# Two attention mixers rewritten: heads in pairs on halves of the array, query norms in the exponent's scale, output units between the pairs

## Chip, core and metric

The kernel runs on one core of one Trainium2 chip. The time is that of the device for one execution, in microseconds; the median of the runs is what counts. TensorE is PE (its weight load PEld), VectorE is DVE, ScalarE is ACT, GpSimd is POOL, SyncE is SP.

## What is computed

Two transformer stacks one after the other on a stream of 256 tokens by 1024 features. The change touches only the mixer of the first stack, which runs twice (two layers). Cut to the mixer:

```python
proj = h @ w_in[l]                      # 1024 -> 1888
a, b_q, b_k, b_v, c, d_cq, d_ckv, d_kr = split(proj)
# a: gated, depthwise convolution of 31 taps, layer norm, silu
o_a = silu(layer_norm(conv31(a[:256] * sigmoid(a[256:])), ln_a_g, ln_a_b))
# b: 4 query heads of 64, 2 key/value heads, RMS norm of q and k, rotary
q = rope_2d(rms_norm(b_q, qk_norm_q)); k = rope_2d(rms_norm(b_k, qk_norm_k))
o_b = softmax(q k^T / 8) v
# c: spatial gating
u, s = gelu(c); s = layer_norm(s) * g + b; o_c = u * (sgu_w @ s + sgu_b)
# d: latent attention, 4 heads of 64 + 32 rotary features
qd = rms_norm(d_cq, mla_q_norm) @ w_uq; kvd = rms_norm(d_ckv, mla_kv_norm) @ w_ukv
o_d = softmax(q_full k_full^T / sqrt(96)) v_d
h = layer_norm(alpha * h + concat(o_a, o_b, o_c, o_d) @ w_out)
```

All is float32. The large projections split each operand into a high and a low float32r part and take three matmuls per product (hi*hi, hi*lo, lo*hi).

## The kernel before

Every engine has its own program in hand-written order, and semaphores tie them together. `mixer(l)` exists once per engine.

**Weights.** They come in units of 128 x 2048 floats (1 MB) in a ring of three buffers. A unit is loaded by SP when the unit three before it has been split; ACT's `split()` copies the raw unit to `w_hi` (line 1473), DVE's `split()` subtracts it to give `w_lo` (line 2038), and PE uses both. ACT's and DVE's splits stand in program order among all their other work, and the n-th split of DVE waits for the n-th of ACT. A mixer has eight input units (`in0` to `in7`, order `IN_ORDER`), one raw unit with the small latent and gating weights (`mla`), four output units (`out0` to `out3`, order `OUT_ORDER`), and then the feed-forward's `gate0` and `up0`.

**Input side.** PE makes `a`, its gate, `q`, `k`/`v`, the latents `cq` and `ckv`, `u` and `sv` (lines 681 and 690, 48 or 72 matmuls each). ACT copies `q`, `k` and the latents out of PSUM and squares them; PE sums the squares with constant matrices (1039, 1041, 1054 to 1056); ACT takes square roots; DVE takes reciprocals of 128 x 768 and 128 x 512 (2436, 2445) and scales `q`, `k` and the latents. Then come rotary matmuls (1061 to 1068), transposes of the gating weights (1079), latent up-projections (1086 to 1101) and their rotary part (1109, 1112), which DVE finishes (2038, from 139 to 144.7 us in the first mixer).

**Attention.** Eight heads go one by one: PE scores (979, two matmuls), DVE maximum (2373) and its negative (2378), ACT exponent with the sum (1689), DVE reciprocal and scaling of the probabilities (2384, 2387), PE transposes (990), ACT copy, PE values (1003), ACT result into `mix`. Behind heads 0 to 4 DVE lays the last 18 of the 30 convolution taps that follow the first (`more_taps`, 2035: a tap is two operations of 128 x 256, and a turn of the loop is two taps), PE lays the gating product `branch_c` behind head 2 (1126, 1127) and the mean and variance of branch a behind heads 5 and 8 (1135, 1142).

**Output.** After the last head `out_rows` runs the four output units (833, 24 matmuls of 128 x 512 each) in the order 1, 2, 0, 3: unit k takes two tiles of `mix`, which DVE splits into `act_hi` and `act_lo` (`split_operand`, 2073 and 2038). Tiles 0 and 1 are branch a, 2 and 3 the heads of b, 4 and 5 branch c, 6 and 7 the heads of d.

## Time and profile before

| | us |
|---|---|
| median of 3 runs | 1941.95 (1940.13 to 1942.10) |
| profiled execution, its own time | 1947.68 |
| its span | 1945.9 |
| PE busy | 1867.0 (96%) |
| DVE busy | 1265.8 (65%) |
| ACT busy | 898.9 (46%) |
| POOL busy | 109.9 (6%) |
| granted TensorE clock, mean | 0.975 |

PE's share is high, but "busy" counts a matmul at half clock as much as one at full clock. The first mixer runs from 74 to 213 us, the second from 413 to 551 us, 339 us later and alike to within a microsecond. Where several engines hand small pieces to each other, the time is read from the order of the pieces, not from the shares.

### The profile page before, as it was taken

The numbers are of one execution on the slowest core, as the hardware profiler recorded it, in microseconds if no ns is written. First come the engines' busy times: TensorE is split into PE (matmuls) and PEld (weight loads), VectorE is DVE, ScalarE is ACT, GpSimd is POOL, SyncE is SP. The second block draws the span as 40 slices with busy tenths as digits, with TensorE's granted clock in tenths as the row PEclk, the third lists the DMA queues.
The fourth block names the chain that finished last, engine by engine and source line by source line (L and its number), as shares of the span: only waits on it lengthen the run. The fifth ranks groups of instructions, "written<-read, shape, count | busy, mean of one in ns | idle before, by whom it ended". The sixth has DMA issues, their size and how long they took to land.

```text
span 1945.9 us, 31345 instructions
## 1 busy us (share of the span) xinstructions
PE 1867.0 (96%) x12538; PEld 1681.6 (86%) x12551; DVE 1265.8 (65%) x1569; ACT 898.9 (46%) x1082; POOL 109.9 (6%) x79
## 2 busy tenths in 40 slices
PE   6988999998999998999999999999999998899999
PEld 6975899987589997999898888999999987789998
DVE  5786877788787677555667655555655567556555
ACT  5544544444454445333554455333433357545332
POOL 0300200030020000000034000000000000000000
PEclk9996999999699999999999999999999998999999
DMA  9540465554046554555442544555555542335553
GB/s 299 187 140 13 145 223 178 175 162 147 8 146 217 193 176 134 191 193 177 132 148 87 202 166 138 188 193 180 177 194 176 190 152 87 110 107 174 183 183 129
DMA packets 227044, 311.34 MB, mean 160 GB/s; under 512 B 6614, under 2 KB 199414, under 8 KB 226326
## 3 DMA queue, kind: packets, MB, share of 16 engines
q1 hardware_dynamic: 224038, 298.07, 45.9%
q0 software_dynamic: 2640, 10.66, 1.7%
q10 hardware_dynamic: 288, 1.54, 0.2%
q8 instruction: 54, 0.88, 0.2%
q14 instruction: 24, 0.20, 0.0%
HBM read 307.09 MB, written 3.15 MB: 159 GB/s over the span
## 4 chain that ended last, share of the span: by engine, by line
PE 88%; DVE 6%; ACT 4%; issue 2%; DMA 1%; DVEq 0%; ACTq 0%
PE bank L681 46%; PE bank L937 18%; PE bank L833 7%; PE bank L704 4%; PE bank L690 3%; PE bank L1003 1%; PE bank L979 1%; PE bank L737 1%; DVE w_lo L2038 1%; DVE work L2035 1%; ACT w_hi L1473 1%; DVE work L2038 1%; PE bank L990 1%; DVE x L2035 1%; PE bank L1127 1%
## 5 line engine op out<-in xcount | busy, mean ns | idle before, releaser
L2038 DVE TENSOR_TENSOR w_lo<-raw,w_hi 128x2048 fp32r<-128x2048 f32 x280 | 643.5, 2307 | 343.7 <-ACT w_hi L1473 343.2
L1473 ACT ACTIVATE w_hi<-raw 128x2048 fp32r<-128x2048 f32 x280 | 532.8, 1904 | 675.7 <-PE bank L681 431.9
L681 PE MATMUL bank<-xt_hi,w_hi 128*128 128x256 f32 x2544 | 723.4, 284 | 4.9 <-DVE w_lo L2038 3.3
L681 PE MATMUL bank<-xt_hi,w_lo 128*128 128x256 f32 x2544 | 721.2, 283 | 0.0
L681 PE MATMUL bank<-xt_lo,w_hi 128*128 128x256 f32 x2544 | 721.1, 283 | 0.0
L681 PEld LDWEIGHTS bank<-xt_hi,w_hi 128*128 128x128 f32 x2544 | 489.0, 192 | 9.3 <-issue 3.7
L681 PEld LDWEIGHTS bank<-xt_lo,w_hi 128*128 128x128 f32 x2544 | 489.0, 192 | 2.4 <-issue 0.2
L681 PEld LDWEIGHTS bank<-xt_hi,w_lo 128*128 128x128 f32 x2544 | 488.9, 192 | 0.0
L937 PE MATMUL bank<-w_hi,act_hi 128*128 128x512 f32 x528 | 206.5, 391 | 0.0
L937 PE MATMUL bank<-w_lo,act_hi 128*128 128x512 f32 x528 | 206.2, 390 | 0.0
L937 PE MATMUL bank<-w_hi,act_lo 128*128 128x512 f32 x528 | 205.5, 389 | 0.0
L937 PEld LDWEIGHTS bank<-w_hi,act_lo 128*128 128x128 f32 x528 | 99.1, 188 | 21.2
L937 PEld LDWEIGHTS bank<-w_hi,act_hi 128*128 128x128 f32 x528 | 99.3, 188 | 19.8 <-DVE act_lo L2038 0.9
L937 PEld LDWEIGHTS bank<-w_lo,act_hi 128*128 128x128 f32 x528 | 99.4, 188 | 18.3
L2035 DVE SCALAR_TENSOR_TENSOR work<-bank,par,work 128x255 f32<-128x255 f32 (+2 forms) x212 | 92.0, 477 | 22.6 <-ACT work L1648 16.1
L833 PE MATMUL bank<-w_hi,act_hi 128*128 128x512 f32 x224 | 90.4, 404 | 7.9 <-ACT work L1775 3.0
L1473 ACT ACTIVATE work<-bank 128x512 f32<-128x512 f32 (+6 forms) x92 | 48.2, 544 | 105.9 <-PE bank L990 39.6
L833 PE MATMUL bank<-w_hi,act_lo 128*128 128x512 f32 x224 | 88.5, 395 | 0.0
L833 PE MATMUL bank<-w_lo,act_hi 128*128 128x512 f32 x224 | 88.3, 394 | 0.0
L704 PE MATMUL bank<-xt_hi,w_hi 128*128 128x256 f32 x208 | 61.4, 295 | 16.3 <-DVE xt_lo L2035 8.2
L1648 ACT ACTIVATE work<-bank,par 128x256 f32<-128x256 f32 x88 | 44.6, 557 | 64.5 <-PE bank L681 64.5
L2038 DVE TENSOR_TENSOR work<-work,bank 128x512 f32<-128x512 f32 x46 | 31.7, 689 | 64.1 <-PE bank L681 57.8
(307 smaller groups left out, 2108.6 us busy)
## 6 DMA issues: line engine op xcount, KB each, us to landing
raw<-in_ffn_wi SPq DMA_DIRECT2D x88, 1024.0 KB, 5.1
raw<-in_ffn_w_up SPq DMA_DIRECT2D x44, 1024.0 KB, 5.1
raw<-in_ffn_wo SPq DMA_DIRECT2D x44, 1024.0 KB, 4.9
raw<-in_ffn_w_down SPq DMA_DIRECT2D x22, 1024.0 KB, 5.4
raw<-in_w_in SPq DMA_DIRECT2D x14, 1024.0 KB, 5.4
raw<-in_ssd_in_proj SPq DMA_DIRECT2D x14, 1024.0 KB, 5.2
raw<-in_mem_wkv SPq DMA_DIRECT2D x9, 1024.0 KB, 8.1
raw<-in_w_out SPq DMA_DIRECT2D x8, 1024.0 KB, 5.1
```

The costliest lines, as they stand in the source:

```text
L681: ins = first(mm(dst, w[s][:, k, c0:c0 + m], xt[v][:, k, :], start=k == 0 and p == 0, stop=k == KT - 1 and p == 2))
L690: ins = first(mm(dst, xt[s][:, k, P * tt:P * tt + P], w[v][:, k, c0:c0 + n], start=start and k == 0 and p == 0, stop=k == KT - 1 and p == 2))
L704: ins = first(mm(dst[:, T * j:T * j + T], w[s][:, k, P * j:P * j + P], xt[v][:, k, :], start=k == 0 and j == 0 and p == 0, stop=k == KT - ...
L737: ins = pe.transpose(bank[b][:, T * half + P * tt:T * half + P * tt + P], src[:, tt, P * k:P * k + P], ident)
L833: ins = first(mm(bank[b][:, :], act[s][:, u % 2, r, P * tt:P * tt + P], w[v][:, r, HALF * h:HALF * h + HALF], start=u == 0 and r == 0 and ...
L937: ins = first(mm(bank[b][:, :], act[s][:, c % 2, j, P * tt:P * tt + P], w[v][:, j, HALF * h:HALF * h + HALF], start=False, stop=True, skip ...
L979: ins = mm(bank[b][:, at:at + n], d["q"][t][c], d["k"][c][:, 0:n], start=c == 0, stop=c == len(d["k"]) - 1)
L990: ins = pe.transpose(bank[b][:, dst:dst + P], prob[:, h % 2, d["at"][t] + P * s:d["at"][t] + P * s + P], ident)
L1473: return act.activation(dst, src, ACT.Copy)
L1648: ins = act.activation(dst[:, c % 2, j, :], bank[b][:, T * j:T * j + T], ACT.Identity, scale=par[:, cw, at], bias=par[:, cb, at])
L2035: return dve.scalar_tensor_tensor(out=out, in0=in0, scalar=scalar, in1=in1, op0=op0, op1=op1)
L2038: return dve.tensor_tensor(out=out, in0=in0, in1=in1, op=op)
```

## The change

What it does, in both mixers:

- the norm of the queries is no longer multiplied into them. PE sums their squares per token into 8 columns (and 2 for the latent), ACT takes the root of these, DVE the reciprocal, and the exponent's per-row scale carries it. The gains go in with ACT's copies out of PSUM
- heads go in pairs. The two heads of a pair of b stand on partitions 0 to 63 and 64 to 127 and their score matmuls alternate; the value matmuls of all pairs alternate between columns 0 to 63 and 64 to 127 of one bank
- pairs 0 and 1 (branch b) begin before the last input unit; output units stand behind the scores of pairs 2 and 3, and after pair 3
- branch a goes last (`OUT_ORDER` 1, 2, 3, 0), and 6 of the 15 turns of taps stand behind the operand of the third output unit
- the gating product uses one bank in place of two.

```diff
-OUT_ORDER = (1, 2, 0, 3)
+OUT_ORDER = (1, 2, 3, 0)
@@ PE
-                claim(4, f"{t}.qms")
-                mm(bank[4][:, :], cst("mean64"), g_sq[:, 0:2, :], start=True, stop=True).then_inc(bank_full[4], 1)
+                claim(6, f"{t}.qss")
+                for j in range(2):
+                    for tt in range(TT):
+                        at = 4 * j + tt
+                        ins = mm(bank[6][:, at:at + 3:2], g_sq[:, j, P * tt:P * tt + P], cst("mean64")[:, 0:P:64],
+                                 start=True, stop=True)
...
+                def scores(p):
+
+                    for i in range(2):
+                        claim(i, f"{t}.s{p}{i}")
+                    for tt in range(TT):
+                        for i in range(2):
+                            dst = bank[i][:, T * tt:T * tt + T]
+                            if p < 2:
+                                r = 64 * i
+                                ins = mm(dst, g_q[r:r + 64, p, P * tt:P * tt + P], g_k[r:r + 64, p, :],
+                                         start=True, stop=True)
...
+                def outputs(p):
+                    for i in range(2):
+                        taken(f"{t}.p{p}{i}")
+                    claim(2, f"{t}.o{p}")
+                    for s in range(TT):
+                        for i in range(2):
...
+                            ins = mm(bank[2][64 * i:64 * i + 64, 0:T], v, prob_t[:, i, T * s:T * s + T],
+                                     start=s == 0, stop=True, skip_group_check=True)
...
+                pe.wait_ge(rot_ready, seen.next(rot_ready))
+                scores(0)
+                pair_tm(f"in{l}.5", 7, f"{t}.sv")
...
+                scores(1)
...
+                turn_probs(0)
...
+                outputs(0)
+                turn_probs(1)
+                outputs(1)
+                branch_c()
...
+                scores(2)
+                out_banks(f"{t}.out")
+                out_rows_of(0)
+                scores(3)
+                out_rows_of(1)
+                turn_probs(2)
+                outputs(2)
+                turn_probs(3)
+                outputs(3)
+                out_rows_of(2)
+                mean_a()
+                variance_a()
+                finish_rows(f"{t}.out", out_unit(units, 3))
@@ ACT, from the exponents on
+                turned_pair(0)
                 act.wait_ge(var_ready, seen.next(var_ready))
                 act.activation(sd[:, 0:TT], mv[:, :, 1], ACT.Sqrt, bias=eps[:, 0:1]).then_inc(sd_ready, 1)
...
+                result(0)
+                turned_pair(1)
+                result(1)
+                split()
+                exponentials(2)
+                split()
+                exponentials(3)
+                turned_pair(2)
+                result(2)
+                turned_pair(3)
+                result(3)
+                split()
+                squares_a()
                 deviation_a()
                 split()
                 activate_a()
-                out_rows(3)
+                split()
@@ DVE
-                step(dve.reciprocal(g_sd[:, :, :], g_sd[:, :, :]))
+                step(dve.reciprocal(g_sd[:, 2, :], g_sd[:, 2, :]))
...
+                maxima(0)
+                split()
+                finish(0)
+                value_stats()
+                maxima(1)
+                more_taps(13, 1)
+                value_norm()
+                finish(1)
+                split()
+                latent_rope()
+                operand(0, "o0", "o1")
+                maxima(2)
+                more_taps(15, 1)
+                gate_c()
+                operand(1, "c")
+                split()
+                finish(2)
+                maxima(3)
+                more_taps(17, 1)
+                finish(3)
+                split()
+                operand(2, "o2", "o3")
+                more_taps(19, 6)
+                dve.memset(st[:, 34:35], 0.0).then_inc(conv_ready, 1)
+                center_a()
+                split()
+                scale_a()
+                dve.wait_ge(branch_a, l + 1)
+                operand(3)
```

DVE at the end of the first mixer, before: the scaled probabilities of the last head (2387), the operands of two output units, a weight split, then branch a's scaling (2508) and its operand.

```order
L2387 TENSOR_SCALAR work<-work,rsum 128x256 x2
L2073 CAST act_hi<-mix 128x512
L2038 TENSOR_TENSOR act_lo<-mix,act_hi 128x512
L2073 CAST act_hi<-mix 128x512
L2038 TENSOR_TENSOR act_lo<-mix,act_hi 128x512
L2038 TENSOR_TENSOR w_lo<-raw,w_hi 128x2048
L2508 RECIPROCAL work<-work 128x256
L2038 TENSOR_TENSOR work<-work 128x512
L2073 CAST act_hi<-mix 128x512
L2038 TENSOR_TENSOR act_lo<-mix,act_hi 128x512
```

And now the same place: the probabilities of pair 3 (2595), the split of the fourth output unit, the operand of the third, the loop of six turns of taps (2526, four operations a turn, of which one is shown), the mean of branch a taken off (2148 out of a bank), a split, and its scaling (2639).

```order
L2595 TENSOR_SCALAR work<-work 128x256 x3
L2148 TENSOR_TENSOR w_lo<-raw,w_hi 128x2048 [waits hi_ready]
L2183 CAST act_hi<-mix 128x512 [waits unit_passed,bank_drained2]
L2148 TENSOR_TENSOR act_lo<-mix,act_hi 128x512 [waits vec_step]
L2526 UNCONDITIONAL_BRANCH
...
L2145 SCALAR_TENSOR_TENSOR work<-work,par 128x256
...
L2148 TENSOR_TENSOR work<-work,bank 128x512 [waits bank_full0]
L2148 TENSOR_TENSOR w_lo<-raw,w_hi 128x2048 [waits hi_ready]
L2639 RECIPROCAL work<-work 128x256 [waits bank_drained1]
L2148 TENSOR_TENSOR work<-work 128x512 [waits vec_step]
L2183 CAST act_hi<-mix 128x512 [waits unit_passed,branch_a]
```

The taps have moved behind the third operand, and a split stands ahead of that operand and another ahead of the scaling.

ACT at the same place, before: the last head's transposed probabilities and result, the deviation of branch a (1775), a split (`w_hi`), the silu (1780).

```order
L1473 ACTIVATE work<-bank 128x512 [waits bank_full3]
L1473 ACTIVATE mix<-bank 128x256 [waits bank_full5]
L1775 ACT_TABLE_LOAD
L1775 ACTIVATE work<-bank,eps 128x256 [waits bank_full7]
L1473 ACTIVATE w_hi<-raw 128x2048 [waits unit_passed,landed1]
L1780 ACT_TABLE_LOAD
L1780 ACTIVATE mix<-work,par 128x256 [waits anorm_ready]
```

And now: both probabilities and the result of pair 3, the split of the fourth output unit, the square and the deviation of branch a (1851, 1855), the split of `gate0`, the silu (1860).

```order
L1556 ACTIVATE work<-bank 128x512 [waits bank_full2]
L1556 ACTIVATE work<-bank 128x512 [waits bank_full3]
L1556 ACTIVATE mix<-bank 128x256 [waits bank_full2,even_rows]
L1556 ACTIVATE w_hi<-raw 128x2048 [waits unit_passed,landed2]
L1851 ACTIVATE work<-work 128x512 [waits bank_drained0]
L1855 ACT_TABLE_LOAD
L1855 ACTIVATE work<-bank,eps 128x256 [waits bank_full1]
L1556 ACTIVATE w_hi<-raw 128x2048 [waits unit_passed,landed0]
L1860 ACT_TABLE_LOAD
L1860 ACTIVATE mix<-work,par 128x256 [waits anorm_ready]
```

The square and deviation stood among the heads and now stand behind the last result, with a split on either side.

DVE in the middle of the mixer now: the probabilities of pair 1, a split, the seven operations of the latent rotary part (32 partitions), the operand of the first output unit, the maxima of pair 2, one turn of taps, the gating product.

```order
L2595 TENSOR_SCALAR work<-work 128x256 x3
L2148 TENSOR_TENSOR w_lo<-raw,w_hi 128x2048 [waits hi_ready]
L2148 TENSOR_TENSOR work<-bank,con 32x512 [waits bank_full6]
...
L2148 TENSOR_TENSOR work<-work 32x1024
L2183 CAST act_hi<-mix 128x512 [waits bank_drained2]
...
L2581 TENSOR_REDUCE work<-bank 128x2 [waits bank_full0]
...
L2145 SCALAR_TENSOR_TENSOR work<-work,par 128x256 [waits vec_step] x4
...
L2148 TENSOR_TENSOR mix<-bank,work 128x512 [waits bank_full5,vec_step]
```

Before, the latent rotary part ended ahead of the first head, and the gating product stood behind head 5.

## Rows read from the trace of the kernel before

**Rows 1.** Busy us by stretch, both mixers; columns PE, PEld, DVE, ACT, POOL, PEclk, DMA, GB/s.

```profile
105.80:140.24 34.44, 33.77 (x204) 25.71 (x202) 27.60 (x29) 18.23 (x26) 0.00 (x0) 1.00 0.25 82
140.24:190.59 50.35, 40.89 (x137) 23.00 (x137) 36.44 (x93) 18.28 (x50) 2.52 (x2) 0.63 0.16 59
...
479.24:529.00 49.76, 40.36 (x136) 22.62 (x136) 36.52 (x93) 18.20 (x50) 2.52 (x2) 0.66 0.16 60
```

**Rows 2.** Granted clock by stretch, PE alone; columns PE busy, PEclk, DMA share, GB/s.

```profile
140.00:142.00 2.00, 0.24 (x2) 0.77 0.97 389
...
170.00:178.00 8.00, 8.00 (x23) 0.50 0.00 0
178.00:180.00 2.00, 2.00 (x10) 0.85 0.00 0
...
1638.00:1640.00 2.00, 2.00 (x7) 0.62 0.00 0
```

**Rows 3.** Timeline of PE, first mixer; start, us, line, tile, form, count, idle before.

```profile
119.08 0.70 PE L1054 MATMUL bank<-work,con 128*128 128x256 f32 x2 [0.37 <-ACT work L1744]
...
144.78 2.09 PE L979 MATMUL bank<-work 64*128 64x256 f32 x8 [4.54 <-DVE work L2038]
149.57 2.07 PE L979 MATMUL bank<-work 64*128 64x256 f32 x4 [2.71 <-ACT work L1689]
...
163.78 0.69 PE L1126 MATMUL bank<-work 128*64 128x128 f32 x2
...
181.34 0.60 PE L990 MATMUL bank<-con,work 128*128 128x128 f32 x4
181.88 1.08 PE L1003 MATMUL bank<-work 128*64 128x256 f32 x4
...
190.59 0.47 PE L833 MATMUL bank<-w_hi,act_hi 128*128 128x512 f32 x1 [1.51 <-ACT work L1775]
...
212.22 0.39 PE L833 MATMUL bank<-w_hi,act_lo 128*128 128x512 f32 x1
```

**Rows 4.** Timeline of PE, sliding-window attention, one pair's outputs.

```profile
1624.09 0.87 PE L1364 MATMUL bank<-work 128*64 128x256 f32 x8
```

**Rows 5.** Timeline of DVE, first mixer.

```profile
138.99 0.69 DVE L2038 TENSOR_TENSOR work<-bank,con 32x512 f32<-32x512 f32 x1 [4.28 <-PE bank L1109]
...
146.89 0.69 DVE L2373 TENSOR_REDUCE rmax<-bank 128x2 f32<-128x512 f32 x1 [1.20 <-PE bank L979]
147.61 0.85 DVE L2378 TENSOR_SCALAR nmax<-rmax 128x2 f32<-128x2 f32 x1
...
159.55 0.62 DVE L2387 TENSOR_SCALAR work<-work,rsum 128x256 f32<-128x256 f32 x2
160.08 3.34 DVE L2035 SCALAR_TENSOR_TENSOR work<-work,par 128x256 f32<-128x256 f32 x8
...
192.06 2.29 DVE L2038 TENSOR_TENSOR w_lo<-raw,w_hi 128x2048 fp32r<-128x2048 f32 x1 [4.46 <-ACT w_hi L1473]
194.27 1.75 DVE L2508 RECIPROCAL work<-work 128x256 f32<-128x256 f32 x1
...
197.90 0.43 DVE L2073 CAST act_hi<-mix 128x512 fp32r<-128x512 f32 x1 [1.16 <-ACT mix L1780]
```

**Rows 6.** Timeline of ACT, first mixer.

```profile
148.50 0.47 ACT L1689 ACTIVATE work<-bank,nmax 128x256 f32<-128x256 f32 x1 [0.29 <-DVE nmax L2378]
...
152.72 0.60 ACT L1473 ACTIVATE work<-bank 128x512 f32<-128x512 f32 x1 [2.29 <-PE bank L990]
...
188.46 1.28 ACT L1775 ACT_TABLE_LOAD   x1
...
190.12 1.90 ACT L1473 ACTIVATE w_hi<-raw 128x2048 fp32r<-128x2048 f32 x1
...
196.78 1.09 ACT L1780 ACTIVATE mix<-work,par 128x256 f32<-128x256 f32 x2 [3.45 <-DVE work L2038]
```

**Rows 7.** Timeline of POOL, first mixer.

```profile
147.18 1.26 POOL L2893 TENSOR_TENSOR work<-work 128x512 f32<-128x512 f32 x1
```

More of the change, by code:

```diff
@@ new lines, in mixer, with out_rows_of @@
+                claim(4, f"{t}.mkr")
+                mm(bank[4][0:96, 0:T], rot, m_kr[64:96, :], start=True, stop=True).then_inc(bank_full[4], 1)
+                outputs(0)
+                turn_probs(1)
+                outputs(1)
+                branch_c()
+                units = [f"out{l}.{j}" for j in OUT_ORDER]
+                def out_rows_of(u):
+                    rows_of = out_unit(units, u)
+                    for tt, h in ORDER:
+                        rows_of(tt, h)
+                taken(f"{t}.mv")
@@ L1769, in squares_a, with turned_pair, result @@
+                def turned_pair(p):
+                    for i in range(2):
+                        b = full(f"{t}.p{p}{i}")
+                        drained(f"{t}.p{p}{i}", copy(prob_t[:, i, :], b[:, :]))
+                def result(p):
+                    act.wait_ge(even_rows, seen.next(even_rows))
+                    b = full(f"{t}.o{p}")
+                    drained(f"{t}.o{p}", copy(mix[:, 2 + p if p < 2 else 4 + p, :], b[:, 0:T]))
                 def squares_a():
@@ L2399, in mixer @@
                 t = f"m{l}"
-                for _ in range(3):
-                    split()
+                split()
+                split()
                 taken(f"{t}.ag")
@@ L2484, in mixer @@
[L2484 to L2495 removed]
+                taken(f"{t}.qss")
@@ new lines, in finish @@
+                def finish(p):
+                    slot = p % 2
+                    for i in range(2):
+                        taken(f"{t}.s{p}{i}")
+                    step(dve.reciprocal(p_rsum[:, slot, :, :], p_expsum[:, slot, :, :]))
+                    for i in range(2):
+                        for tt in range(TT):
+                            part = pair_prob[slot][:, i, T * tt:T * tt + T]
+                            ins = dve.tensor_scalar(part, part, p_rsum[:, slot, i, tt:tt + 1], None, ALU.mult)
+                    ins.then_inc(prob_ready, 1)
```

351 lines of the change are left out of this document (194 added, 157 removed).

## The prediction

> **What bounds the kernel now.** I read the busy time by stretch first. From 105.8 to 140.24 us PE has work for 33.77 of 34.44 us at full clock; from there to the first output unit it is busy 40.89 of 50.35 us, but at a mean granted clock of 0.63, and mixer 2 shows the same 50 us at 0.66 [rows 1]. The clock by stretch then shows that it falls to 0.5 right after PE runs dry at 140.24 and stays there, with PE "busy" 8.00 of 8.00 us from 170 to 178, until just after 178 [rows 2]: small float32 matmuls in a row did not bring it back there. In the sliding-window stage it came back within about 3 us of a dense output unit (0.62 in the mean of 1638 to 1640) [rows 2]. So the 50.35 us are a chain of hand-overs on a half-speed PE. At full clock that stretch holds some 27 us of PE work: 16 score matmuls and 16 value matmuls (1.0 us for two, by L1003 at 181.88), eight times four transposes (0.53), branch c (16 at 0.31, half of the 0.62 from start to start of L1126 and L1127 at the low clock), mean and variance 2.0 [rows 3]. The output units are 22 us of dense PE work, 5.5 us each (from 190.59 to 212.6) [rows 3]. If PE never waited, there would be 23 us a mixer to win. Whether the change wins them depends on DVE and ACT, so I walk its order engine by engine with the durations of now.
>
> **The small edits.** Pairs: the first eight records of L979 are two heads on different partitions issued back to back, and take 2.09 us at the low clock, where one head alone takes 2.07 [rows 3]. So two heads of b cost what one costs (about 1.05 us at full clock, 2.1 at half). For values on column halves, four matmuls of 768 columns in sum take 0.87 us in the other stage [rows 4], so 1024 columns take 1.1 against 2.0 apart. The scores of the latent pairs use 96 rows and win nothing (2.0 a pair, 4.1 at low clock). On DVE the reciprocals shrink from 768 and 512 columns to 256 each (1.75 us for 256 [rows 5]), some 5 us in all, but ahead of the heads, where PE is not waiting for DVE: nothing. ACT gets two more table loads of 1.28 us [rows 6]; only the one before the deviation of `sv` is on a path. The loads of the output units keep their triggers, and the third now waits for `mv`, 30 us before ACT wants it: nothing.
>
> **Step 1, up to the probabilities of pair 1 (mixer 1).** PE has the work of now up to 140.24, plus two pair scores (2.1), transposes and values of pair 0 (2.1), less 0.7 of idle: it stands at 143.8. DVE is later. The scores of pair 0 end at 123.8 (rotations 2.6 and sums 1.2 are now ahead of `u`, which ended 0.37 before 119.08 [rows 3]), maxima 1.5, exponents 1.85 (four of 0.47 with their sums [rows 6]): 127.2. From there the order is a chain: ACT split 1.9 [rows 6], DVE split 2.2 [rows 5] (it stands ahead of `finish(0)`), `finish` 1.5 (four of 0.31 and a reciprocal [rows 5]), statistics 0.95, maxima 1.55 (0.69 each [rows 5]), exponents 1.85, five copies 2.6 and two of the turned probabilities 1.15 (0.60 long, every 0.5 [rows 6]), table load and root 1.6, normalization 0.9, `finish` 1.5. Sum 17.75: 145.0. POOL's two multiplications for branch c start just before that last `finish`. In the trace DVE's 128 x 2 operation at 147.61 takes 0.85 us where its neighbours take 0.17, and ends with POOL's instruction of 147.18 to 148.44 [rows 5, 7]. I take that for a block and add 2.1: 147.1.
>
> The Trainium skill ("SBUF — State Buffer", "Who interferes with whom") says that VectorE in a two-port mode and GpSimd exclude each other for a whole instruction, whoever issues first. By it the block is certain; by the row alone it is likely; without it the time would be 2.1 us a mixer less.
>
> **Step 2, to the first output unit.** From 143.8 PE waits 3.3 us after a run of light matmuls, longer than before the clock fell at 141. I take the low clock until dense work comes. Turn 2.1, copies 0.6, values 1.9, result 0.4, then ACT's split 1.9 (it stands behind `result(1)`), DVE's split 2.2, the latent rotary part 5.7 (from 138.99 to 144.7 [rows 5]), scores of pair 2 4.1, the last maximum 0.9, one turn of taps 1.7 (3.34 for two [rows 5]), `gate_c` 0.7, since `out_banks` claims the bank that it empties. Sum 22.2: 169.3. Branch c (9.9 at low clock) lies beside the splits and the rotary part.
>
> **Step 3, to the result of pair 3.** Unit 0 5.5 and 1.5 for about 3 us at the low clock, scores 2.0, unit 1 5.5, twice turn 1.05, copies 0.6, values 1.05, result 0.4 (3.1). Sum 20.7: 190.0. The DVE work here (operand, split, `finish(2)`, maxima, taps, `finish(3)`) is shorter than the PE work beside it.
>
> **Step 4, the third operand.** ACT's split of the fourth unit stands behind `result(3)`, DVE's split before the operand: 1.9 and 2.2 and 1.1 (a cast of 0.43 and a subtraction of 0.69, the form of 138.99 [rows 5]). PE idles 5.2 us, to 195.2. Today the corresponding operands are ready within 1.5 us of the last head.
>
> **Step 5, taps.** Six turns, 24 operations at 0.417: 10.0 us, to 205.2. Unit 2 (7.0 with the clock coming back) covers 7.0 for PE, but mean and the rest wait for the taps. Today all taps are over at 177.8, behind the heads.
>
> **Step 6, branch a.** Mean 1.0, centering 0.7, square 0.6, variance 1.0, root 0.45, ACT split 1.9, DVE split 2.2, reciprocal 1.75 and scaling 0.65 [rows 5], silu 1.1 [rows 6], operand 1.1. Sum 12.45: 217.7. PE has nothing in most of it. Step 7: the last unit 5.5 and 1.5 for the clock: 224.7. Now it ends at 212.6. **The sum** is +12.1 us a mixer, +24.2 for both, with nothing to change behind them. The profiled execution had 1947.68 us (span 1945.9), the median is 5.7 lower; I add the sum to the median: 1966.
>
> **Costs that the trace doesn't show** and their bounds: the column halves (0.87 measured on a shorter form; from no gain, +1.0 a pair and 4 a mixer, to the whole gain, which I take because the same form is there); the eight narrow sums of squares (0.1 to 0.3 each; on PE ahead of the heads, under 1 us); the clock in step 2 (at full clock 4.0 less, worked out below).
>
> **Rivals.** *A, the clock holds.* PE's idle time before pair 1 is shorter than I think, or the block doesn't come, and step 2 runs at full clock: turn 1.05 less, values 0.85 less, scores 2.1 less, unit 0 1.5 less, block 2.1 less: 7.6. Then +4.5 a mixer and 1951; with the block, +6.6 and 1955. For it: dense units surround the heads, and before 140.24 light matmuls ran at full clock. Against it: the fall at 141 and 37 us without recovery [rows 2]. *B, faster: the splits are not on the chain.* I put three splits of ACT and DVE (4.1 us a pair, in steps 2, 4 and 6) in series with PE's results. If ACT is ahead of PE there, so that its half is done earlier, and DVE's runs beside PE, 12.3 us of them vanish, and with A's 7.6 the mixer is 7.8 shorter: 1926. It decides from 12.1 us of the chain up. Against it stands the order: `w_hi` follows `result(3)` on ACT, and nothing passes it there. *C, the halves don't run together* in the pairs, each serial: 4 for values and 2 for scores a mixer, 1978. Against: the 2.09 of [rows 3]. *D, it does nothing:* what PE gains by pairs and by early units equals what the end loses, within 4 us. It needs A and shorter ends of steps 5 and 6 by 3 us or more a mixer.
>
> The Trainium skill ("TensorE: Matmul & The Clock Gate", Part 4: PE-mode transpose) says that transposes do not count as busy for the clock. That bears on A: turning the probabilities would not hold the clock, whatever PE's busy share; this trace agrees in that it shows 0.5 beside a full busy share, though it can't name the transposes as the cause. By that rule A would be left with the time before pair 1's transposes alone.
>
> **How the numbers follow.** Forecast (1959 to 1975) 0.58; A (1950 to 1958) 0.22; C and worse 0.06; D 0.05; B 0.09. The likeliest gives 1966. The range takes the forecast and A, 0.80 together: 1950 to 1976. A measurement of this kernel can tell about 0.2% (3.9 us) from no change. Faster by more 0.09, within it 0.05, slower by more 0.86.
>
> **What would show it.** In the changed profile: DVE at a standstill ahead of three `w_lo` splits with ACT's `w_hi` as releaser (steps 2, 4, 6); some 10 us of taps right behind the third operand while PE finishes its unit and stops; the granted clock low from about 143 to 172 and again around 195 and 218 in the first mixer; the last output unit ending 10 to 14 us later, and the second mixer like the first. Wrong would be a first output unit before 165 (A), or PE busy through branch a's chain (B). If the L1124 values of a pair take 2 us at full clock, C holds.

## The result

| | before | after |
|---|---|---|
| median, us | 1942.03 (1940.13 to 1946.07, 4 runs) | 1983.48 (1978.52 to 1984.78, 4 runs) |
| profiled execution, its own time | 1947.68 | 1978.52 |
| its span | 1945.9 | 1976.7 |
| granted TensorE clock, mean | 0.975 | 0.968 |

One execution of a kernel below (re-timed, units last) took 4611 us, in a slow state; all medians are of fast executions alone.

The ratio is 1.0215, with a 95% interval of 1.0199 to 1.0231: slower by 41.5 us, where the forecast was +24 and the range ended at 1976. The two profiled executions are 30.8 us apart. The missing 17 us are therefore two things: 7 between the forecast and the two traces, and 11 between the profiled executions and the medians (5.7 for the kernel before, 5.0 for the changed one). Both are accounted for below.

The profile page's list of the costliest groups shows the kind of loss in one line. The columns are line, engine, operation, tiles, shape and count, then busy us and mean ns, then the idle time before. It is the first of three matmul groups of all output units, in the kernel before and in the changed one:

```profile
L833 PE MATMUL bank<-w_hi,act_hi 128*128 128x512 f32 x224 | 90.4, 404 | 7.9 <-ACT work L1775 3.0
```

```profile
L843 PE MATMUL bank<-w_hi,act_hi 128*128 128x512 f32 x224 | 95.9, 428 | 41.8 <-DVE act_lo L2148 32.4
```

The group counts all output units of the kernel, of which eight are those of the two mixers. TensorE waits 34 us longer ahead of output units, nearly all of it for `act_lo`, the operand that DVE splits.

TensorE's timeline of the changed kernel, first mixer, is to be laid beside [rows 3]. L1113 turns probabilities, L1124 multiplies by the values, L1100 makes latent scores, L843 is an output unit, L1147 and L1154 are the mean and the variance of branch a, L768 is the next stage. Three points stand for rows left out:

```profile
147.18 1.97 PE L1113 MATMUL bank<-con,work 128*128 128x128 f32 x8 [3.62 <-DVE work L2595]
149.88 1.97 PE L1124 MATMUL bank<-work 128*64 128x256 f32 x8 [0.73 <-ACT work L1556]
...
162.08 3.75 PE L1100 MATMUL bank<-work 96*128 96x256 f32 x8 [0.59 <-issue]
169.19 0.77 PE L843 MATMUL bank<-w_hi,act_hi 128*128 128x512 f32 x1 [3.36 <-issue]
...
188.65 1.08 PE L1124 MATMUL bank<-work 128*64 128x256 f32 x8 [0.78 <-ACT work L1556]
195.46 0.80 PE L843 MATMUL bank<-w_hi,act_hi 128*128 128x512 f32 x1 [5.72 <-DVE act_lo L2148]
...
205.55 1.51 PE L1147 MATMUL bank<-work,con 128*128 128x256 f32 x4 [2.55 <-DVE st L2673]
208.51 2.07 PE L1154 MATMUL bank<-work,con 128*128 128x256 f32 x4 [1.44 <-ACT work L1851]
219.97 0.79 PE L843 MATMUL bank<-w_hi,act_hi 128*128 128x512 f32 x1 [9.39 <-DVE act_lo L2148]
...
227.30 1.89 PE L768 MATMUL bank<-zero 128*128 128x512 bf16 x8
```

What to look for: only some rows carry a wait in brackets, and the last four waits (5.72, 2.55, 1.44 and 9.39 us) stand between the last values (188.65) and the last unit. The next stage starts at 227.30; in the kernel before the last unit ended at 212.6 [rows 3].

DVE's timeline of the same mixer shows who was late:

```profile
143.83 3.30 DVE L2595 TENSOR_SCALAR work<-work 128x256 f32<-128x256 f32 x4
...
154.17 2.29 DVE L2148 TENSOR_TENSOR w_lo<-raw,w_hi 128x2048 fp32r<-128x2048 f32 x1 [7.04 <-ACT w_hi L1556]
...
192.06 2.29 DVE L2148 TENSOR_TENSOR w_lo<-raw,w_hi 128x2048 fp32r<-128x2048 f32 x1 [9.16 <-ACT w_hi L1556]
...
195.33 10.04 DVE L2145 SCALAR_TENSOR_TENSOR work<-work,par 128x256 f32<-128x256 f32 x24
...
212.92 2.29 DVE L2148 TENSOR_TENSOR w_lo<-raw,w_hi 128x2048 fp32r<-128x2048 f32 x1 [5.13 <-ACT w_hi L1556]
215.13 1.75 DVE L2639 RECIPROCAL work<-work 128x256 f32<-128x256 f32 x1
```

Three times it stands still (7.04, 9.16 and 5.13 us) ahead of a `w_lo` for which ACT's `w_hi` is not ready, and between two of them it has 10 us of taps in a row. The busy time by stretch, against [rows 1] (columns: busy us of PE, PEld, DVE, ACT and POOL, then PEclk, DMA share and GB/s):

```profile
140.24:190.59 50.35, 39.00 (x158) 25.35 (x158) 26.02 (x46) 17.13 (x34) 2.52 (x2) 0.73 0.25 84
190.59:228.50 37.91, 19.59 (x62) 13.94 (x64) 24.34 (x43) 11.48 (x11) 0.00 (x0) 0.68 0.17 56
```

In the first stretch the clock is higher than in [rows 1] (0.73 against 0.63) and two output units are already inside it. The second holds the other two units, 11 us of work, in 38 us. The signs that the prediction named are all there: the three waits of DVE, the taps in a row, and a clock of 0.59 in 144 to 148, 0.50 in 148 to 172 and 194 to 199, and 0.51 or less in 206 to 222. Only the last unit ends 14.6 us later, where it said 10 to 14.

### The profile page after: what moved, and what is told of

The parts are those of the page before. It is cut to its first block, busy times and chain, and to the rows that moved or that the text cites. A ratio compares the mean times of both kernels' runs of the same rounds, so it can differ in the third digit from the quotient of the medians.

```text
span 1976.7 us, 31350 instructions
## 1 busy us (share of the span) xinstructions
PE 1858.6 (94%) x12558; PEld 1683.4 (85%) x12571; DVE 1257.8 (64%) x1550; ACT 903.0 (46%) x1088; POOL 110.2 (6%) x79
## 4 chain that ended last, share of the span: by engine, by line
PE 87%; DVE 5%; ACT 5%; issue 2%; DMA 0%; DVEq 0%; ACTq 0%
PE bank L691 46%; PE bank L947 18%; PE bank L843 7%; PE bank L714 4%; PE bank L700 3%; PE bank L747 1%; ACT w_hi L1556 1%; DVE work L2145 1%; ACT work L1556 1%; DVE w_lo L2148 1%; PE bank L989 1%; PE bank L1100 1%; PE bank L1013 1%; DVE x L2145 1%; PE bank L1140 0%
## 5 line engine op out<-in xcount | busy, mean ns | idle before, releaser
L947 PE MATMUL bank<-w_hi,act_hi 128*128 128x512 f32 x528 | 206.6, 391 | 0.0
L947 PE MATMUL bank<-w_lo,act_hi 128*128 128x512 f32 x528 | 206.2, 391 | 0.0
L843 PE MATMUL bank<-w_hi,act_hi 128*128 128x512 f32 x224 | 95.9, 428 | 41.8 <-DVE act_lo L2148 32.4
L947 PEld LDWEIGHTS bank<-w_hi,act_hi 128*128 128x128 f32 x528 | 99.3, 188 | 19.9 <-DVE act_lo L2148 0.9
L843 PEld LDWEIGHTS bank<-w_hi,act_hi 128*128 128x128 f32 x224 | 45.6, 203 | 56.9 <-DVE act_lo L2148 35.5
L843 PE MATMUL bank<-w_lo,act_hi 128*128 128x512 f32 x224 | 92.3, 412 | 0.0
L843 PE MATMUL bank<-w_hi,act_lo 128*128 128x512 f32 x224 | 91.9, 410 | 0.0
L714 PE MATMUL bank<-xt_hi,w_hi 128*128 128x256 f32 x208 | 61.5, 296 | 16.2 <-DVE xt_lo L2145 8.1
```

What stands on the lines that cost most here:

```text
L714: ins = first(mm(dst[:, T * j:T * j + T], w[s][:, k, P * j:P * j + P], xt[v][:, k, :], start=k == 0 and j == 0 and p == 0, stop=k == KT - ...
L843: ins = first(mm(bank[b][:, :], act[s][:, u % 2, r, P * tt:P * tt + P], w[v][:, r, HALF * h:HALF * h + HALF], start=u == 0 and r == 0 and ...
L947: ins = first(mm(bank[b][:, :], act[s][:, c % 2, j, P * tt:P * tt + P], w[v][:, j, HALF * h:HALF * h + HALF], start=False, stop=True, skip ...
```

## The experiments

All times are medians; the ratio to the kernel before has its interval in brackets. "Period" is the time from the gate of the first mixer to that of the second, read from ACT's sigmoid in each trace. It holds one mixer and the stage behind it, and is 339.6 us before and 354.4 after (start of the first and of the second sigmoid):

```profile
L1713 ACT ACTIVATE work<-bank x2: 597/598/598, 86.2 to 425.8; 128x512 f32<-128x512 f32 x2
```

```profile
L1796 ACT ACTIVATE work<-bank x2: 598/598/598, 86.0 to 440.4; 128x512 f32<-128x512 f32 x2
```

A period is that of one execution. Two executions of one kernel differed in it by 5.1 and by 1.9 us (last two rows), so a few us of period are no effect by themselves.

| kernel | us | ratio | period |
|---|---|---|---|
| taps early | 1976.05 | 1.0178 (1.0161 to 1.0195) | 351.0 |
| taps and branch a early | 1956.08 | 1.0073 (1.0056 to 1.0090) | 341.7 |
| splits early | 1966.27 | 1.0131 (1.0114 to 1.0148) | 347.3 |
| zeros in the wait for pair 1 | 1979.25 | 1.0189 (1.0172 to 1.0206) | 354.5 |
| kernel before, with zeros | 1944.40 | 1.0020 (1.0007 to 1.0033) | 333.3 |
| re-timed | 1925.31 | 0.9917 (0.9900 to 0.9933) | 324.7 |
| re-timed, units last | 1933.94 | 0.9956 (0.9940 to 0.9971) | 332.5 |
| re-timed, branch c first | 1914.65 | 0.9860 (0.9840 to 0.9881) | 319.6 |
| pair 1 finished first | 1972.93 | 1.0165 (1.0143 to 1.0186) | 350.7 |
| kernel before again | 1942.43 | 0.9997 (0.9985 to 1.0008) | 334.5 |
| changed kernel again | 1983.31 | 1.0206 (1.0176 to 1.0235) | 356.3 |

**Step 5, the taps.** The changed kernel with its last taps moved into DVE's gaps:

```diff
                 maxima(1)
-                more_taps(13, 1)
+                more_taps(13, 4)
                 value_norm()
                 finish(1)
+                more_taps(21, 4)
...
-                more_taps(15, 1)
+                more_taps(29, 1)
+                dve.memset(st[:, 34:35], 0.0).then_inc(conv_ready, 1)
...
-                more_taps(17, 1)
...
-                more_taps(19, 6)
-                dve.memset(st[:, 34:35], 0.0).then_inc(conv_ready, 1)
```

> The changed kernel, with the last taps of branch a moved on DVE into its idle times before the output units (4 turns behind the maxima of pair 1, 4 behind finish(1), 1 behind the maxima of pair 2); nothing else moves. Theory (the end is a chain of waits, each of its own size): the taps cost only the 2.9 us by which they outlast the third output unit (PE stands from 202.6 to 205.5 in mixer 1), and a mean at low clock: 3 to 5 us a mixer, 1973 to 1977. Rival (the 10 us of taps are on the path in full): 20 us less, 1963. Rival (the size lies in the clock, not in the waits): under 2 us in all.

1976.05 us, 7.4 less than the changed kernel and inside the theory's 1973 to 1977. TensorE's timeline of this kernel:

```profile
202.74 1.02 PE L1147 MATMUL bank<-work,con 128*128 128x256 f32 x4
205.21 1.13 PE L1154 MATMUL bank<-work,con 128*128 128x256 f32 x4 [1.44 <-ACT work L1851]
215.82 0.79 PE L843 MATMUL bank<-w_hi,act_hi 128*128 128x512 f32 x1 [9.48 <-DVE act_lo L2148]
```

The mean no longer waits, the last unit starts 4.15 us earlier, and the wait ahead of it is the same 9.4 us. So the taps cost what they outlasted the third unit by, not their 10 us, and the step behind them is untouched.

**Steps 6 and 7, branch a.** The same, with the mean, variance, root, silu and scaling of branch a ahead of the third output unit on all three engines, of which TensorE's part is:

```diff
                 scores(3)
+                mean_a()
                 out_rows_of(1)
+                variance_a()
                 turn_probs(2)
...
                 out_rows_of(2)
-                mean_a()
-                variance_a()
```

> e1_taps, and branch a's mean and variance on PE behind the scores of pair 3 and the second output unit, its square, root and silu on ACT and its scaling on DVE ahead of the third operand. Theory: the last unit follows the third at once; of the 17.4 us from the end of the third to the start of the last (202.6 to 220.0) all goes but 2 us for mean and variance that now stand ahead, and the last unit no longer starts at the low clock (1.5): 15 to 17 us a mixer, 1949 to 1953, still over the kernel before by 7 to 11 us, which is what steps 2 to 4 cost. Rival (branch a's chain is only late because everything before it is, and a new wait takes its place): under 10 us a mixer, above 1963.

1956.08 us, 3 above the upper end of what was expected. In TensorE's timeline the third unit now starts later, the fourth directly behind it, and the next stage 13.2 us earlier:

```profile
200.69 0.79 PE L843 MATMUL bank<-w_hi,act_hi 128*128 128x512 f32 x1 [8.13 <-DVE act_lo L2148]
...
214.10 2.10 PE L768 MATMUL bank<-zero 128*128 128x512 bf16 x9
```

The silu with its table load now stood between the last result and ACT's split, which lengthened the wait for the third operand from 5.72 to 8.13 us. A step taken off the path was partly paid for by one put on it, on the same engine.

**Steps 4 and 6, ACT's splits.** The changed kernel with the fourth unit's split ahead of the turned probabilities, and the next stage's split behind the silu:

```diff
                 exponentials(3)
+                split()
                 turned_pair(2)
                 result(2)
                 turned_pair(3)
                 result(3)
-                split()
...
-                split()
                 activate_a()
+                split()
```

> The changed kernel, with ACT's split of the fourth output unit ahead of the turned probabilities of pair 2 (it stood behind the last result), and both halves of the split of gate0 behind branch a's silu and scaling. Theory (the splits are in series with PE's results): 4.1 us less before the third operand and 4.1 us less in branch a's chain, 8.2 a mixer, but the taps (10.0 us from the third operand on) keep their distance: 1966 to 1968. Rival (ACT could not have split earlier, since the raw unit or the buffer is not free): no change, 1983.

1966.27 us, as expected by the theory. The waits ahead of the last two units fall from 5.72 and 9.39 us to 1.78 and 5.39:

```profile
191.37 0.79 PE L843 MATMUL bank<-w_hi,act_hi 128*128 128x512 f32 x1 [1.78 <-DVE act_lo L2148]
...
211.21 0.80 PE L843 MATMUL bank<-w_hi,act_hi 128*128 128x512 f32 x1 [5.39 <-DVE act_lo L2148]
```

Rival B of the prediction held that the splits are not on the chain. Moving two of its three gave 17 us; these two are on it.

**Step 2, the clock.** The changed kernel with 15 matmuls on zeros (extra work, no output changed) in TensorE's wait for pair 1:

```diff
                 outputs(0)
+                keep_busy(3, 15)
                 turn_probs(1)
```

> The changed kernel with 15 matmuls of zeros (128x512, 0.23 us each, 3.4 us in all) on PE in the 3.6 us in which it waits for the probabilities of pair 1. Theory (the waits set the time, the clock adds): the clock holds, and turn 0.9, values 0.9, scores of pair 2 1.9 and the first unit 1.4 get faster on the path, 4 to 5 us a mixer: 1973 to 1975. Rival (the clock is what the forecast missed): 15 us or more in all, 1968 or less, with a smaller spread of the runs. Rival (light matmuls alone let the clock fall): it falls anyway within the pair's work, 0 to 3 us in all.

1979.25 us: below the changed kernel by 4, between the 8 or more of the theory and the 0 to 3 of the last rival. TensorE's timeline and the clock by stretch:

```profile
147.38 1.09 PE L1113 MATMUL bank<-con,work 128*128 128x128 f32 x8 [0.28 <-DVE work L2596]
149.26 1.08 PE L1124 MATMUL bank<-work 128*64 128x256 f32 x8 [0.79 <-ACT work L1557]
160.57 3.75 PE L1100 MATMUL bank<-work 96*128 96x256 f32 x8 [4.64 <-issue]
```

```profile
150.00:156.00 6.00, 5.93 (x36) 3.03 (x32) 3.30 (x3) 2.18 (x2) 0.00 (x0) 1.00 0.01 3
156.00:158.00 2.00, 0.00 (x0) 0.00 (x0) 2.00 (x4) 0.00 (x0) 0.00 (x0) 0.58 0.83 266
158.00:172.00 14.00, 8.07 (x18) 6.00 (x19) 11.07 (x18) 5.38 (x10) 0.00 (x0) 0.50 0.11 37
```

The zeros did what they were for: the turned probabilities took 1.09 us in place of 1.97, and branch c ran at full clock. TensorE then came to the scores of pair 2 at 155.9, 5.6 us earlier than in the changed kernel, and stood 4.64 us, and the clock fell there. The row names no releaser; on DVE's timeline the latent rotary part, for which these scores wait, ends at 160.5. So what branch c gained from the clock went into this wait; what turning and multiplying pair 1 gained (1.8 us) came through, and the first unit started 1.5 us earlier (167.69). That was nearly lost again inside this unit, whose matmuls ran at the low clock for 5.7 us from its start, and for 3.0 in the first trace of the changed kernel. The period of this trace is no shorter than the one there (354.5 and 354.4 us) and 1.8 shorter than that of the second trace. The same in the kernel before:

```diff
+                taken(f"{t}.mv")
+                keep_busy(1, 18)
                 pe.wait_ge(rot_ready, seen.next(rot_ready, 2))
```

> The kernel before, with 18 matmuls on zeros put into TensorE's queue in front of the first head, once the latent value bank is drained, in the stretch in which the engine idles or does light work. They are extra work and change no output. Theory that the clock alone makes the stretch from 141 to 178 us of the kernel before slow: that stretch ran at 0.5 for about 37 us with TensorE busy some 26 of them, so up to 12 us a mixer could come back, about 1918 us in all. Rival: the waits between the engines set the stretch and the clock falls again at the first wait of a few microseconds, as it did in the run with zeros in the changed kernel: 0 to 4 us a mixer, 1934 to 1942 us. The zeros may also stand in front of the first head by up to 2 us: then up to 1946 us.

1944.40 us, slower by 0.2%: the rival, and nothing gained. TensorE's timeline shows that the zeros end before DVE's rotary part does, so they are not on the path, and that the first scores run at full clock:

```profile
139.69 3.83 PE L758 MATMUL bank<-zero 128*128 128x512 bf16 x17 [0.16 <-issue]
144.07 1.14 PE L979 MATMUL bank<-work 64*128 64x256 f32 x8 [0.55 <-DVE work L2040]
147.65 2.07 PE L979 MATMUL bank<-work 64*128 64x256 f32 x4 [2.44 <-ACT work L1691]
```

Behind the next wait the clock is down. The period of 333.3 us looks like 6 us won against the first trace of the kernel before (339.6), and is 1.2 against its second (334.5, below); the second mixer with its next stage took 344.4 us here and 341.1 there. Zeros in a wait were worth 4 us in the one kernel and nothing in the other; where the 2.8 us between these medians come from is not shown.

**Step 1.** The changed kernel with two lines exchanged on DVE:

```diff
-                value_norm()
                 finish(1)
+                value_norm()
```

> The changed kernel with one line moved: on DVE pair 1 is divided by its sums ahead of the normalization of the gated values, and not behind it. It undoes step 1 of the prediction alone (the wait for ScalarE's root at 142.8 and the block by GpSimd no longer stand ahead of pair 1's probabilities). Theory (the steps are one chain): probabilities of pair 1 turned at about 144.1 in place of 147.2, everything up to the first output unit 3 to 4 us earlier, and so the mixer's end; 6 to 8 us in all, about 1975 us. If the clock also holds without that wait, scores of pair 2 come 4 us earlier: 1974 us. Rival (the end is set by the taps on DVE and what follows them, step 5, which do not hang on pair 1): 1980 to 1984 us.

1972.93 us, 10.6 less, more than the 6 to 8 of the plain theory and near the 1974 with the clock holding. DVE's row of that kernel, against 3.30 us at 143.83 above, and TensorE's:

```profile
137.74 1.14 DVE L2595 TENSOR_SCALAR work<-work 128x256 f32<-128x256 f32 x4
```

```profile
143.91 1.06 PE L1113 MATMUL bank<-con,work 128*128 128x128 f32 x8 [0.66 <-ACT mix L1556]
145.76 1.08 PE L1124 MATMUL bank<-work 128*64 128x256 f32 x8 [0.78 <-ACT work L1556]
157.07 3.75 PE L1100 MATMUL bank<-work 96*128 96x256 f32 x8 [4.28 <-issue]
```

The division takes a third of the time when GpSimd has nothing to do, and pair 1 is turned 3.3 us earlier. It is also turned and multiplied at full clock (1.06 and 1.08 us, where the changed kernel took 1.97 for each), which is 1.8 us more, and the first output unit starts at 164.18, 5.0 us earlier. The clock fell in the 4.28 us of the next wait (0.50 in 153 to 157). So of these 5.0 us, 3.3 are step 1 and the rest is the clock of pair 1. The Trainium skill ("SBUF — State Buffer", "Who interferes with whom") says that VectorE's two-port modes and GpSimd exclude each other; the trace agrees, with 3.30 against 1.14 us for the same four instructions, though it does not show the mode.

**All steps together.** If the steps are places where one engine's written order makes the others wait, a list written from the traces should undo them all and leave what pairs save. The main moves:

```diff
                 maxima(1)
-                more_taps(13, 1)
-                value_norm()
+                more_taps(13, 2)
                 finish(1)
-                split()
+                more_taps(17, 1)
+                value_norm()
                 latent_rope()
...
                 scores(3)
+                branch_c()
+                turn_probs(2)
+                outputs(2)
+                turn_probs(3)
                 out_rows_of(1)
-                turn_probs(2)
-                outputs(2)
-                turn_probs(3)
+                mean_a()
                 outputs(3)
+                variance_a()
                 out_rows_of(2)
-                mean_a()
-                variance_a()
```

> The changed kernel with its heads still in pairs and its output units still between the pairs, and the written lists re-timed from the traces so far. DVE: pair 1 is finished ahead of the value norm, the latent rotary part stands directly behind the value norm, taps fill the waits, branch a's mean comes before the last operand by two units. TensorE: scores of pair 2 and the first output unit ahead of branch c, the first unit of scores of pair 3 ahead of branch c too, turned probabilities of pairs 2 and 3 ahead of the second output unit, the mean behind it, the variance ahead of the third. ScalarE: the splits of the last two units no longer stand in the chain. Theory (my steps 1 to 7 all are places where one engine's written order makes the others wait, and pairs as such save work): by a walk over the durations of the trace the mixer's last unit ends at 190 to 195 us in place of 227.2, so 32 to 37 us a mixer, 1910 to 1920 us, faster than the kernel before by 1 to 1.6%. Rival (the work of the stretch is bound by TensorE at its low clock or by the sum of DVE's work, not by the written order): under 20 us a mixer, 1944 us or more.

1925.31 us: 58 less than the changed kernel and 0.8% faster than the kernel before, 5 above what the walk gave (the last unit of the first mixer ends at 195.8). In the stretch of the mixer TensorE is now busy 49.37 of 56 us at a mean granted clock of 0.85:

```profile
140.00:196.00 56.00, 49.37 (x213) 34.95 (x213) 43.44 (x75) 27.45 (x42) 3.40 (x2) 0.85 0.30 102
```

The kernel before was not re-timed in the same way. So the 0.8% are shown for the pairs, the early units and the new lists together, and not for the pairs alone.

**Units laid between.** The same kernel with all four units behind the attention; one split on ACT and one on DVE moved back a step with them:

```diff
-                out_banks(f"{t}.out")
-                out_rows_of(0)
                 scores(3)
...
-                out_rows_of(1)
                 mean_a()
                 outputs(3)
+                out_banks(f"{t}.out")
+                out_rows_of(0)
+                out_rows_of(1)
                 variance_a()
```

> The re-timed kernel of the same job with all four output units behind the attention (the first two no longer between the pairs). Theory: with the rest re-timed, the two units between the pairs fill waits of TensorE that now stand empty, of about 5 to 9 us a mixer, and hold the clock up: 10 to 18 us over the re-timed kernel. Rival: the units laid between only push branch a's and pair 3's steps back by what they take: within 3 us of the re-timed kernel, or faster than it.

1933.94 us, 8.6 above the re-timed kernel; the theory wanted 10 to 18, the rival at most 3. Up to the values of pair 2 the waits stand empty (TensorE is busy 28.76 of 36 us), and the clock is low:

```profile
140.00:176.00 36.00, 28.76 (x98) 15.74 (x96) 30.04 (x59) 15.69 (x31) 3.39 (x2) 0.56 0.34 117
```

So laying units between the pairs is worth some 9 us, about half a per cent, in this list. Whether it was worth as much in the changed kernel's own list was not tried.

**Branch c in the wait.** The re-timed kernel with branch c ahead of the scores of pair 2, where TensorE had stood 2.94 us, and the second unit right behind the turned probabilities of pair 2. That is where the changed kernel already had branch c. Some splits, taps and maxima on ACT and DVE were laid anew with it:

```diff
                 outputs(1)
+                branch_c()
...
                 scores(3)
-                branch_c()
                 turn_probs(2)
+                out_rows_of(1)
                 outputs(2)
                 turn_probs(3)
-                out_rows_of(1)
-                mean_a()
                 outputs(3)
+                mean_a()
                 variance_a()
```

> The re-timed kernel with branch c ahead of the scores of pair 2 (its matmuls in the wait that TensorE has there, and at the full clock), the second output unit directly behind the turned probabilities of pair 2, the values of pairs 2 and 3 behind that unit, the split of the last unit ahead of the second result. Theory (a wait filled with the light matmuls of branch c takes them out of the stretch at 0.5): branch c takes about 5.9 us in place of 9.9, and the mixer's last unit ends at about 190.5 in place of 195.8, so 10 us less in all than the re-timed kernel, about 1915 us. Rival (the light work brings the clock down wherever it stands, and the scores of pair 2 now come 3 us later on the chain): no gain or up to 6 us lost, 1925 to 1931 us.

1914.65 us, where 1915 was expected: 1.4% faster than the kernel before and 3.5% faster than the change. The last unit ends at 192.0 in the first mixer, 106.1 us behind the gate, where the re-timed kernel has 111.3. How these 5 us a mixer divide among the moves is not shown.

**The baseline.** Both kernels unchanged, for a second trace of each:

> The kernel before, unchanged, for a second profiled execution. The first had a granted clock of 0.975 and 1947.68 us, where 20 other runs had 0.978 to 0.982 and 1937.6 to 1944.0 us. Theory (the first profiled run was one with an unusually low clock in the mixers, and so my durations of before were too long against its median): a span of 1936 to 1942 us at 0.979 to 0.982, with the first mixer's output units starting 3 to 7 us earlier than at 190.59. Rival (the extra time of that run lay in other stages): the mixer's rows again within 1 us of the first ones, while the span is shorter by 4 us or more. If the span is again 1945 us or more, the profiler itself costs it.

> The changed kernel, unchanged, for a second profiled execution: the first had 1978.52 us at 0.968, the three others 1982.3 to 1984.8 us at 0.966. Theory (the runs differ by where the clock rises again in a mixer): a span of 1980 to 1984 us with the mixer's steps up to 4 us later than in the first trace. Rival (the runs differ in later stages): the mixers' rows within 1 us of the first ones.

The first theory holds for the kernel before: a span of 1941.3 us at 0.981, and in TensorE's timeline the first output unit at 186.42, where [rows 3] has 190.59, although this mixer began 0.9 us later. L990 turns probabilities, L1126 belongs to branch c:

```profile
156.13 1.11 PE L990 MATMUL bank<-con,work 128*128 128x128 f32 x4 [0.64 <-DVE work L2387]
...
162.98 0.43 PE L1126 MATMUL bank<-work 128*64 128x128 f32 x2
...
186.42 0.47 PE L833 MATMUL bank<-w_hi,act_hi 128*128 128x512 f32 x1 [1.51 <-ACT work L1775]
```

```profile
158.00:160.00 2.00, 2.00 (x5) 1.07 (x4) 1.97 (x5) 0.00 (x0) 0.00 (x0) 0.50 0.00 0
160.00:162.00 2.00, 1.99 (x11) 1.09 (x11) 1.93 (x8) 1.30 (x5) 0.00 (x0) 0.81 0.02 4
162.00:167.00 5.00, 5.00 (x30) 2.48 (x28) 4.90 (x15) 1.72 (x6) 0.00 (x0) 1.00 0.02 3
...
169.00:174.00 5.00, 5.00 (x14) 3.04 (x13) 3.30 (x11) 1.51 (x5) 0.00 (x0) 0.50 0.00 0
174.00:176.00 2.00, 2.00 (x11) 1.30 (x9) 1.06 (x4) 0.60 (x1) 0.00 (x0) 0.90 0.00 0
```

The same instructions in the same order. In the first trace the clock stayed at 0.5 until 178 [rows 2] and two matmuls of branch c took 0.69 us; here it rose at 161, fell at 168 and rose again at 175, and they took 0.43. Its period is 334.5 us, not 339.6, and the second mixer with the stage behind it is 4.2 us shorter too (341.1 against 345.3 us from the gate to the first silu of the stage after). Against these 9.3 us stand the start, 0.9 later, and 3.8 us that everything behind took longer (3.4 of them up to the gate of the state-space stage), which leaves the 4.6 between the spans.

Of 45 executions of the kernel before whose clock is on record beside that of the first profiled one, 42 had 0.978 or more and at most 1944.0 us; three had 0.975, as it had, and 1945.7 to 1945.8 us. One more, whose clock is not on record, took 1946.07 us. So the profiled execution was one of a rarer kind, four or five in 50. Whether the others of this kind lost their time in the mixers too, no trace shows.

For the changed kernel neither theory holds alone. The second trace began 1.5 us earlier; the first period is 1.9 us longer, the second mixer with its next stage 0.8, and what lies behind again 3.8, together the 4.9 us between the spans, to 0.1. Most of the 1.9 lies between the first unit's start and the values of pair 2, here 17.29 us and in the first trace 15.90 (169.19 to 185.09); the first unit's matmuls ran at the low clock for 6 us here and for 3 there:

```profile
167.71 0.76 PE L843 MATMUL bank<-w_hi,act_hi 128*128 128x512 f32 x1 [3.36 <-issue]
...
185.00 1.08 PE L1124 MATMUL bank<-work 128*64 128x256 f32 x8 [0.78 <-ACT work L1556]
```

## Why the prediction was right in direction and short in size

Two terms of it failed. The baseline: the sum compared with one trace of the kernel before and was added to the median, whose mixers are shorter (9.3 us for both). And step 6: mean and variance were priced at full clock and ran at the low one (2.0 us a mixer with the hand-overs). The mechanism, a chain of waits that the written order makes, held.

The walk against the first trace, first mixer, us:

| step | predicted | measured |
|---|---|---|
| 1, pair 1's probabilities | 147.1 | 147.1 |
| 2, first output unit | 169.3 | 169.2 |
| 3, result of pair 3 | 190.0 | 190.2 |
| 4, third operand | 195.2 | 195.4 |
| 5, end of the taps | 205.2 | 205.5 |
| 6, last operand | 217.7 | 219.9 |
| 7, end of the last unit | 224.7 | 227.2 |

**Steps 1 to 5 held** to 0.3 us, and the experiments that took one of them away gave its worth: step 1, with the clock of pair 1, 10.6 us in all, the splits of steps 4 and 6 17, the taps of step 5 7.4. GpSimd's block was where step 1 put it (2.16 us, 3.30 less 1.14, against 2.1). Small errors inside cancelled: four exponents with their sums take 2.3 us and not 1.85, the scores of pair 2 3.75 and not 4.1. (The terms of step 1 add up to 17.7, where it says 17.75.)

**Step 6 was mis-sized.** It took 14.4 us (205.5 to 219.9) in place of 12.45. I had priced the mean and the variance at full clock, 1.0 each, although the same step says that TensorE has nothing to do in most of it; they took 1.51 and 2.07 at the low clock. That is 1.6; the other 0.4 are hand-overs between engines, for which the sum had nothing. With step 7 that makes a period 14.8 longer in place of 12.1. The second mixer with its next stage became 16.2 us longer (361.5 against 345.3), so the two come to 31.0 us, beside 30.8 between the first spans.

**The baseline was the larger error.** The sentence "I add the sum to the median" assumed that a mixer of the profiled execution is a mixer of the median. The second trace of the kernel before, whose own time (1943.06 us) lies near the median, shows that it was not: its two mixers were 5.1 and 4.2 us shorter. The "37 us without recovery" at half clock [rows 2] were those of an execution of the rarer kind. Its 5.7 us above the median were in sight and I wrote them down, but as a constant offset, and not as time that might lie in the very stretch on which every step of the sum rested. The sum from 24 to the result is then: 24.2 forecast, 6.8 in the steps, 9.3 by which the mixers of the kernel before were shorter in its second trace, 2.7 by which the changed kernel's were longer in its second trace: 43.0, less 2.6, by which the changed kernel came to its first gate earlier (84.5 against 87.1 us). The second spans are 40.3 us apart (1981.6 and 1941.3), the medians 41.5. One trace a kernel carries these figures, so their split is good to a microsecond or two.

**The rivals.** A (the clock holds) fell: in the changed kernel the clock went down ahead of pair 1 and came back with the first unit. But the experiment with zeros, where it held up to the scores of pair 2, gave 2 us a mixer by it, not the 5.5 that were left of A's 7.6 with the block: the scores of pair 2 and the first unit ran at the low clock even so. B fell by the early splits, C by the 1.08 us of L1124 at 188.65 (a pair's values at full clock, as taken from [rows 4]), and D with the result.

**What is not settled** is why the clock rises in one execution and not in another with the same instructions, why everything behind the mixers took 3.8 us longer in both second traces than in the first, and what each kernel would take at a steady clock: the zeros held it in neither kernel up to the first output unit.

## What to carry to other kernels

When work of one engine is laid between that of others, walk every other queue in the new order: here a kernel with the same pairs and early units is 1.4% faster than the one before, and what made it 2% slower was the place of a few lines, of which those tested alone stand on DVE and ACT (a split behind the last result, taps gathered behind the last operand, a division behind a root that it does not need). Before adding a sum to a median, look whether the profiled execution's own time and granted clock are those of the median. Where they are not, the difference may sit in the stretch that is being changed.

## What the runs showed of the hardware

The clock can fall without a wait just before. In the kernel with branch c first TensorE was busy without a gap from 147.3, and after branch c's small matmuls the clock went down around 153:

```profile
146.00:152.00 6.00, 5.76 (x34) 3.00 (x34) 5.90 (x10) 2.18 (x2) 1.27 (x1) 1.00 0.02 6
152.00:154.00 2.00, 2.00 (x9) 1.24 (x9) 1.97 (x3) 0.00 (x0) 0.00 (x0) 0.69 0.00 0
154.00:158.00 4.00, 4.00 (x11) 3.18 (x10) 2.53 (x5) 1.28 (x1) 0.00 (x0) 0.50 0.45 134
```

The next scores took 3.78 us in place of 1.89, and in the unit behind them the clock came back (0.80 in the mean of 158 to 162, 1.00 from 162 on). The Trainium skill ("TensorE: Matmul & The Clock Gate", Part 4: PE-mode transpose) says that transposes do not count as busy; the last transposes here ended at 145.2, 8 us ahead of the fall, so that rule alone does not explain it. In the second trace of the kernel before the clock rose in the middle of such light work (0.50 in 158 to 160, 1.00 in 162 to 167). In the kernel with branch c first, light matmuls laid into a wait left a slow stretch themselves, but did not hold the clock for the scores that followed.
